# Dividing the softmax weights by their sums on GpSimd instead of VectorE, in a two-network transformer kernel

## The reference, cut to what matters

```python
# first block, layer 0: chunk_attention, 8 heads of 64
s = einsum('bnihd,bnkhd->bnhik', qc, kb) * (d ** -0.5) + bias      # masked to the chunks so far
p = softmax(s); o = einsum('bnhik,bnkhd->bnihd', p, vb)
# second block, layer 0: forgetting attention (8 heads) and sparse attention (8 heads, two gated branches)
# second block, both layers: memory_cross_attention, 4 heads against 256 memory tokens
s = einsum('bqhd,bmhd->bhqm', q, k) * HEAD_DIM ** -0.5
p = softmax(s); o = einsum('bhqm,bmhd->bqhd', p, v)
```

## Time and profile before

| what | value |
|---|---|
| median of 3 runs | 2141.16 us |
| profiled execution | 2144.88 us, span of the trace 2143.1 us |
| PE busy | 1766.5 us (82%), mean granted clock 0.879 |
| DVE busy | 1353.6 us (63%) |
| ACT busy | 1146.6 us (54%) |
| POOL busy | 7.2 us, 16 instructions |
| a0's attention | about 242 to 290 us |
| b0's attention | about 1363 to 1425 us |
| cross attentions | about 1474 to 1492 and 1901 to 1916 us |

### The profile page before, as it was taken

How to read it: one execution, slowest core, us unless ns; L and a number is a source line. 1 busy time by engine, 2 the same in 40 slices (tenths; PEclk the granted TensorE clock), 3 DMA queues, 4 the chain that set the end, 5 groups by cost and what they waited for, 6 DMA issues and landing times.

```text
span 2143.1 us, 26347 instructions
## 1 busy us (share of the span) xinstructions
PE 1766.5 (82%) x9072; PEld 1470.3 (69%) x9072; DVE 1353.6 (63%) x2051; ACT 1146.6 (54%) x1720; POOL 7.2 (0%) x16
## 2 busy tenths in 40 slices
PE   4496567999998977789999987886799886748997
PEld 3475456888885854578888666654799775538996
DVE  3697775898885656568898743454545454654543
ACT  4232334788873388468788643344444444554443
POOL 0000000000000000000000000000000000000000
PEclk9698677999999956789999998597899997888999
DMA  7585363999994722369999842211365552113651
GB/s 266 196 282 189 124 229 106 349 370 327 330 357 147 268 69 79 128 231 328 353 358 325 306 123 70 79 59 60 102 193 177 176 178 89 61 58 123 191 190 66
DMA packets 219091, 413.24 MB, mean 193 GB/s; under 512 B 14784, under 2 KB 71232, under 8 KB 218608
## 3 DMA queue, kind: packets, MB, share of 16 engines
q1 hardware_dynamic: 214224, 400.74, 54.4%
q10 hardware_dynamic: 3600, 6.90, 0.9%
q0 software_dynamic: 1184, 4.52, 0.7%
HBM read 411.06 MB, written 1.05 MB: 192 GB/s over the span
## 4 chain that ended last, share of the span: by engine, by line
PE 69%; DVE 17%; ACT 8%; issue 4%; ACTq 1%; DMA 0%; DVEq 0%
PE bank L682 20%; PE bank L683 19%; PE bank L684 19%; DVE row_gains L1986 4%; DVE weights_low L1764 3%; PE bank L704 2%; PE bank L865 2%; PE bank L950 1%; ACT features_parts L1301 1%; DVE features_parts L1780 1%; ACT scratch L1403 1%; PE bank L820 1%; DVE normed L1861 1%; DVE x_state L1865 1%; PE bank L789 1%
## 5 line engine op out<-in xcount | busy, mean ns | idle before, releaser
L1764 DVE TENSOR_TENSOR weights_low<-weight_ring,weights_high 128x1024 fp32r<-128x1024 f32 x664 | 781.9, 1218 | 206.8 <-ACT weights_high L1293 123.2
L682 PE MATMUL bank<-weights_high,features_parts 128*128 128x512 f32 (+2 forms) x1520 | 604.0, 397 | 37.0 <-DVE weights_low L1764 9.6
L683 PE MATMUL bank<-weights_low,features_parts 128*128 128x512 f32 (+2 forms) x1520 | 594.6, 391 | 0.0
L684 PE MATMUL bank<-weights_high,features_parts 128*128 128x512 f32 (+2 forms) x1520 | 593.9, 391 | 0.0
L1531 ACT ACTIVATE weights_high<-weight_ring 128x1024 fp32r<-128x1024 f32 x384 | 393.8, 1056 | 107.2 <-PE bank L684 70.0
L682 PEld LDWEIGHTS bank<-weights_high,features_parts 128*128 128x128 f32 x1520 | 290.7, 191 | 104.2 <-DVE weights_low L1764 21.6
L684 PEld LDWEIGHTS bank<-weights_high,features_parts 128*128 128x128 f32 x1520 | 289.7, 191 | 60.5
L683 PEld LDWEIGHTS bank<-weights_low,features_parts 128*128 128x128 f32 x1520 | 290.7, 191 | 56.7 <-issue 0.7
L1293 ACT ACTIVATE weights_high<-weight_ring 128x1024 fp32r<-128x1024 f32 (+1 forms) x184 | 185.0, 1044 | 192.8 <-PE bank L684 101.2
L682 PE MATMUL bank<-features_parts,weights_high 128*128 128x256 f32 x768 | 222.9, 290 | 11.8 <-ACT qk_features L1315 6.3
L683 PE MATMUL bank<-features_parts,weights_high 128*128 128x256 f32 x768 | 221.1, 288 | 0.0
(11 more groups left out here) (318 smaller groups left out, 1656.6 us busy)
## 6 DMA issues: line engine op xcount, KB each, us to landing
weight_ring<-in_exp_w_gate SPq DMA_DIRECT2D x128, 512.0 KB, 5.1
weight_ring<-in_exp_w_up SPq DMA_DIRECT2D x128, 512.0 KB, 5.1
weight_ring<-in_exp_w_down SPq DMA_DIRECT2D x128, 512.0 KB, 5.3
weight_ring<-in_ada_w SPq DMA_DIRECT2D x96, 512.0 KB, 5.0
weight_ring<-in_ffn_wg SPq DMA_DIRECT2D x44, 512.0 KB, 4.2
weight_ring<-in_ffn_wu SPq DMA_DIRECT2D x44, 512.0 KB, 4.8
weight_ring<-in_ffn_wd SPq DMA_DIRECT2D x44, 512.0 KB, 4.2
weight_ring<-in_even_w_in SPq DMA_DIRECT2D x28, 512.0 KB, 5.7
```

Of the source, the lines that this page charges most:

```text
L682: eng.matmul(dst, lh, rh, start=first, stop=False, **kw)
L683: eng.matmul(dst, lh, rl, start=False, stop=False, **kw)
L684: mm = eng.matmul(dst, ll, rh, start=False, stop=last, **kw)
L1764: V(half_of(low(s), i, size), half_of(slot(n), i, size), half_of(high(s), i, size).bitcast(F32), ALU.subtract)\
```

## The change

GpSimd gets a loop over the items of each attention, which waits for the reciprocals, multiplies the four tiles in place and signals after each head. VectorE keeps the reciprocals and gates, whose last instruction now signals `recips_ready`, and goes on without waiting for the scaling. A settling wait between the reciprocals and the scaling, where no gate follows, goes with it. In GpSimd's list the loop for a0 stands ahead of all its DMAs, b0's and ca0's behind the first three row-gain loads, ca1's at the end.

```diff
@@ vector: attention
                     if 1 <= t <= n:
                         d, u, r = pairs.items[t - 1], u0 + t - 1, recips(t - 1)
                         eng.wait_ge(probs_ready, 4 * (u + 1))
-                        eng.reciprocal(r, small(SUMS, t - 1)).then_inc(*vec.up())
-                        settle()
                         if d["kind"] == "nsa":
                             at = 6 * d["p"] + 1 + d["b"]
                             r2 = r.rearrange("p (e t) -> p t e", t=TB)
-                            V(r2, r2, GT[:, :, at:at + 4:3], ALU.mult).then_inc(*vec.up())
+                            eng.reciprocal(r, small(SUMS, t - 1)).then_inc(*vec.up())
                             settle()
-                        for e in range(2):
-                            for tb in range(TB):
-                                p = pairs.probs(t - 1, e)[:, pairs.score_cols(tb)]
-                                ins = eng.tensor_scalar(p, p, r[:, 2 * e + tb:2 * e + tb + 1], None, ALU.mult)
-                            ins.then_inc(probs_scaled, 1)
+                            V(r2, r2, GT[:, :, at:at + 4:3], ALU.mult).then_inc(recips_ready, 1)
+                        else:
+                            eng.reciprocal(r, small(SUMS, t - 1)).then_inc(recips_ready, 1)
@@ gpsimd
+            def scale_probs(pairs):
+                for t, d in enumerate(pairs.items):
+                    u, r = pairs.first + t, recips(t)
+                    eng.wait_ge(recips_ready, u + 1)
+                    for e in range(2):
+                        for tb in range(TB):
+                            p = pairs.probs(t, e)[:, pairs.score_cols(tb)]
+                            ins = eng.tensor_scalar(p, p, r[:, 2 * e + tb:2 * e + tb + 1], None, ALU.mult)
+                        ins.then_inc(probs_scaled, 1)
+            scale_probs(Pairs("a0", pview(EVEN_IN)))
             eng.wait_ge(x_ready, 4)
...
+                if l == 0:
+                    scale_probs(Pairs("b0", pview(EV_IN)))
+                    scale_probs(Pairs("ca0"))
...
+            scale_probs(Pairs("ca1"))
```

More of the change, by code:

```diff
@@ L297, in build @@
         scores_ready, shifted, probs_ready = sem("scores_ready"), sem("scores_shifted"), sem("probs_ready")
+        recips_ready = sem("recips_ready")
         probs_scaled, probs_turned = sem("probs_scaled"), sem("probs_transposed")
```

## The result

| | median us | lowest to highest, runs |
|---|---|---|
| before | 2141.41 | 2138.49 to 2143.38, 4 |
| changed | 2172.37 | 2170.70 to 2174.61, 4 |

The changed kernel takes 1.0143 times as long, 95% interval 1.0128 to 1.0159: 31 us more. I had forecast 2149.1 and a range up to 2163. The direction was right; the size was four times too small, and the range missed it.

A forecast was written before the change was run, and what follows sets the result against it. VectorE was taken to bound a0, and a ring of waits through the scaling b0 from item 3. a0 +3.8, b0's item 0 +0.95, ring +2.7, cross attentions +0.4: +7.9 us on 2141.2, forecast 2149.1, range 2136 to 2163.

The forecast's parts named there:

- the price of GpSimd's four scalings: Time GpSimd needs to scale one item's four tiles, taken from ScalarE's exponentials: 1.86 us, or 2.08 in the cross attentions.
- The bound above: Upper limit for four scalings: each as long as VectorE's 128x512 operation with two large inputs, 751 ns, so 3.0 us.
- GpSimd is slower than I take it: Rival, chance 0.06: GpSimd's scaling takes 2.6 us or more an item, giving 2160 to 2167 us.
- my upper bound of 2167: Whole kernel with 0.3 us of start delay and 3.0 us of scaling an item: +25.8 us, 2167.0.
- Waking up: Delay before GpSimd's first scaling of an item, 0.3 us, from a start beside ScalarE on one signal; bound below 0.
- a0: +3.8 forecast: In a0, VectorE's copy comes 0.95 us later in each of four iterations, with the modulation steps queued behind it.
- b0's ring: b0, items 3 to 11: reciprocals, GpSimd's scaling, head 1's transposes, VectorE's copy; turn 3.90 against 3.56 us, eight times, +2.7.
- b0's first items: Before item 3 in b0: item 0's transposes end 0.95 us later; items 1 and 2 are covered by TensorE's own work.
- Rival 3: Chance 0.09: a longer turn in b0 drops TensorE's clock to 1.2 GHz, eight times 0.8 us more, 2155.5 us.
- Cross attentions: In ca0 and ca1, values start near 1484.73 against 1484.54, +0.2 us each, +0.4 together.
- The second item's scaling ends before TensorE has finished: In ca0 and ca1, GpSimd's second-item scaling is done before TensorE finishes head 0's transposes, so it adds no wait.
- What I said would refute it: Signs against the forecast: the copy does not wait, row minima stretch while GpSimd works, or TensorE's clock falls.

## Why the prediction was wrong

- **The failed step is the price of GpSimd's four scalings.** "The nearest rows are ScalarE's exponentials ... I take these": 1.86 and 2.08 us. Measured: 2.99 and 3.63. The bound above, 3.0 us, was met almost exactly in a0 and b0 and passed in the cross attentions, and I gave "GpSimd is slower than I take it" 6 of 100. At the measured price and start my own sum would be 7.5 + 1.9 + 10.2 + 3.1 = 22.7 us, 2163.9. So this step is 15 of the 23 us that were missing; the rest is a stage and a path that I had wrong, told below, which took the time past my upper bound of 2167 too. ScalarE's duration says nothing of GpSimd's. The honest reading of bounds 1.0 and 3.0, with no row of the engine computing anything, was that either end is as likely as the middle.
- **Waking up.** I took 0.3 us; GpSimd starts 0.1 us after the reciprocals end (1406.40 to 1406.48 in the chain; 0.04 from GpSimd to TensorE behind it). The row of the DMA start that I used shows another kind of instruction.
- **a0: +3.8 forecast, +8.0 measured.** With 2.99 and 0.1 the same sum gives 251.98 + 0.1 + 2.99 + 0.04 + 0.90 + 0.04 = 256.05, 1.88 late, four times 7.5. The modulation steps did start later each time, as said. Mechanism right.
- **b0's ring: +2.7 forecast, +10.0 measured.** With the measured price the turn is 0.42 + 0.10 + 2.99 + 0.04 + 0.55 + 0.04 + 0.69 = 4.83 us; measured 38.22 / 8 = 4.78. Mechanism right; half the columns (30.11 us) confirm it at another price.
- **b0's first items: +0.95 forecast, +5.5 measured.** At the true price the first item is 1.9 late. The other 3.6 us are the clock. Rival 3 had TensorE's clock falling in the ring, where it stayed at 1.00 until 1438, the last turn. (The rival was not idle: in the run with extra transposes the clock did fall in the ring, and one turn took 5.99 us.) It was the items before the ring, where the clock was about to rise, that lost it. I had weighed the stage already at the high level and not the one that had yet to reach it, though the 5.04 us of scores in the earlier trace rows stand there at the low one.
- **Cross attentions: +0.4 forecast, +6.5 measured, and 3.3 behind them.** "The second item's scaling ends before TensorE has finished" was false at 3.63 us: reciprocals are 5.72 us apart against 3.84, because they stand behind the first item's waiting copy, and the second item's scaling is then on the path as well. By the prediction's own path the price alone gives 3.1 for both. Behind ca1 came 2.4 us of clock. The sum with the upper bound had 3.5 for the two, a figure whose working the prediction does not show.
- **The two did not hinder each other** in the changed kernel: GpSimd's longest scaling is 927 ns beside a mean of 923. VectorE's row minima read PSUM and one tile of SBUF.
- **What I said would refute it** ("if the clock falls") was near: up to the ring's last turn it didn't fall, it rose late.

## What to carry to other kernels

Before work moves to an engine that has computed nothing in the trace, no neighbour's duration is its price: keep the range to both bounds, and weigh them evenly. (Here even that range, up to 2167, would have missed, by the clock and the second item of the cross attentions.) Moving work off the busier engine saves nothing where that engine next waits for the same work's result. Find that first waiting instruction, and write the new ring with the price as a variable. Look for stretches in which TensorE is still at 1.2 GHz and busy: a wait of 2 to 3 us put in there was paid again in everything that then ran at the low level (3.6 us in b0, 2.4 behind ca1), and with GpSimd on head 1 alone 0.24 us more of waiting went with the same loss in b0.

## What the hardware showed that I had not expected

- GpSimd's in-place multiplication of f32 tiles by a factor for each row: 442, 604 and 923 ns for 64, 128 and 256 columns, 77 ns less with a constant factor. VectorE takes 279 and about 350 ns for the last two.
- Beside VectorE's modulation steps GpSimd's four tiles take 3.53 us in a0's first two items and 3.90 in its last two, instead of 2.99. The larger tiles take 1200 ns on average instead of 923 and the first small one 746 to 789 instead of 604, but the second small one keeps its 600. VectorE's steps hardly change, 759 ns against 751. The Trainium skill, "SBUF — State Buffer", section "Who interferes with whom", says that a VectorE instruction with two SBUF inputs contends with a GpSimd instruction that reads SBUF; the trace agrees for three of the four tiles, and shows GpSimd as the one that waits. By the same section of the Trainium skill a VectorE instruction with at most one SBUF input doesn't contend, as long as it is not in one of VectorE's two-port modes. The undisturbed 927 ns beside the row minima agree; beside VectorE's own scalings, which also read one tile of SBUF, GpSimd's first tile was longer, 747 ns against 604, and no run shows in which mode those scalings ran.
- The time in which TensorE stays at 1.2 GHz can change by more than the edit does: item 2 to 3 of b0 was either 4.7 to 5.0 us or 8.3 in every run with the copy in its old place, and nothing between: 4.7 to 5.0 with GpSimd out of the first items, 8.3 wherever it had a part in them, even half of it.
